# Expert layer: the 64 sample tokens' experts gathered by index and summed on VectorE, the other 512 tokens dense at 512 columns with the values summed in PSUM

## The chip, the cores and the metric

The kernel runs on one core of a Trainium2 chip. The metric is the device time of one execution in microseconds (us). The engines named below are PE (TensorE; PEld is its weight load), DVE (VectorE), ACT (ScalarE), POOL (GpSimd) and SP (SyncE, which issues the DMAs; SPq is its queue).

## The reference, cut to what matters

Two layers of a decoder trunk run for 512 prompt tokens and 64 sample tokens (576 in all), width 1024. Each layer ends in a product-key expert layer, and only that part is changed:

```python
N_KEYS, N_EXPERTS, PEER_HEADS, PEER_DK, PEER_TOPK = 128, 128 * 128, 8, 128, 16
def block(xb):
    q = (xb @ wq).reshape(blk, PEER_HEADS, 2, PEER_DK)
    s = jnp.einsum('nhpd,hpkd->nhpk', q, keys)
    s1, i1 = lax.top_k(s[:, :, 0], PEER_TOPK)
    s2, i2 = lax.top_k(s[:, :, 1], PEER_TOPK)
    cand = (s1[..., :, None] + s2[..., None, :]).reshape(blk, PEER_HEADS, PEER_TOPK * PEER_TOPK)
    cidx = (i1[..., :, None] * N_KEYS + i2[..., None, :]).reshape(blk, PEER_HEADS, PEER_TOPK * PEER_TOPK)
    sc, pos = lax.top_k(cand, PEER_TOPK)
    idx = jnp.take_along_axis(cidx, pos, axis=-1)
    g = jax.nn.softmax(sc.astype(jnp.float32), axis=-1)
    act = jax.nn.gelu(jnp.einsum('nhkd,nd->nhk', u_tab[idx], xb), approximate=False)
    return jnp.einsum('nhk,nhkd->nd', (g * act).astype(v_tab.dtype), v_tab[idx])
```

Each token picks 128 (8 heads x 16) of 16,384 experts. An expert is one row of `u_tab` and one of `v_tab`, 1024 float32 (4 KB) each.

## The kernel before

The experts are computed densely for all 576 tokens. The 16,384 experts are 128 "rows" (tiles) of 128. All large products are made of three matmuls on a high and a low float32r part (high x high, high x low, low x high). ACT casts the high part, DVE subtracts to get the low part.

**`lookup_stage`** works through 144 tiles of weights: 16 query tiles (`w_query`) and 128 tiles of `u`. A tile is loaded into one of four slots of `raw` by SP, cast to `wh` by ACT (`high`), split to `wl` by DVE (`low`), and multiplied on PE (`product`, `split_product`, L1664): 8 k-blocks x 3 parts x 2 column halves of 288 = 48 matmuls. ACT drains the result from PSUM, through Gelu into `go` for a `u` tile, and SP writes it to the DRAM tensor `activated` (`gd`). A tile's `low` is made three tiles ahead (`LEAD = 3`), and it can only be made after the tile four places earlier is used.

- The *static part* (72 tiles) has the query tiles in pairs, 2 query and 7 `u` tiles for each of 8 heads. After a query tile PE makes `scores` (L1780). DVE runs the top-16 search of a head between the `low`s, in program order: 9 `low`s for a head. At its end DVE makes the softmax weights (`found`, L2011), PE transposes indices and weights (L1819), and DVE copies them to `ix` (L2018).
- The *beats* are 72 more tiles, one with each group of 8 tokens (`GT = 8`). DVE builds one-hot rows in float16 (`one_hots`, L2033 to L2037), PE multiplies them (`sums`, L1789, 8 matmuls of 256 columns: for each token the 128x128 table of its weights, in a high and a low half), ACT copies the high halves to `wt` (L1893) and DVE adds the low halves (L2056). After four beats SP writes 2 MB of `wt` to the DRAM tensor `coefficients` (`wd`).

**`value_stage`** multiplies `activated` by `coefficients` (`weigh`), splits the result into parts, and multiplies with `v` in blocks of 8 rows: for each row 8 column groups of `v` x 3 parts x two column pieces (320 and 256) = 48 matmuls (L2145). A column group takes one and a half PSUM banks, so half the groups are worked on at a time, and after 8 rows DVE adds the sums to `h` in SBUF (`evict`, L2227). SP then writes `h` to `residual` and `y` (L2123, L2124) in two halves; the first half is written while the last half-block is computed. The stage ends when all four writes have landed, and the next layer begins.

Every stage ends in a barrier of all engines.

Of the kernel before, what the change touches and what calls it, by code (L numbers as in the profile page):

```python
# [16 lines left out]
P = 128  # L17
# [9 lines left out]
HALF = N // 2  # L27
H = 4
# [1603 lines left out]
ROWS = 8  # L1632
BLOCKS = NKEY // ROWS
STEPS = 2 * ROWS
HALVES = NKEY // 4
CH = 32
CHUNKS = N // CH
# [6 lines left out]
TILES_STATIC = 2 * PH_HEADS + U_STATIC  # L1644
TILES_ALL = 2 * PH_HEADS + NKEY
PIECES = ((0, 320), (320, 256))
# [12 lines left out]
def split_product(nc, T, out, slot, a):  # L1659

    cols = slice(a * HALF, (a + 1) * HALF)
# [5 lines left out]
    return last  # L1667


def lookup_stage(nc, T, l):  # L1670
# [4 lines left out]
    with stage(nc, "raw0", "raw1", "raw2", "raw3", "keys_in", "high", "low", "used", "drained", "scored", "kept",  # L1675
               "topped", "zeroed", "counted", "cast", "chain_v", "exp_in", "exped", "found", "turned", "tail",
               "g0", "g1", "g2", "g3", "idx_ready", "eq_ready", "rows", "summed", "halved", "evicted", "w_even", "w_odd",
               "normed", "x_high", "x_low", shared=T.bridge) as (block, s):
        raw_in = (s["raw0"], s["raw1"], s["raw2"], s["raw3"])
        g_out = (s["g0"], s["g1"], s["g2"], s["g3"])  # L1680
        w_out = (s["w_even"], s["w_odd"])

        @block.gpsimd
        def _(pool):
            nc.gpsimd.iota(T.iota[:], pattern=[[1, P]], base=0, channel_multiplier=0,
                           allow_small_or_imprecise_dtypes=True).then_inc(s["counted"], 1)

        @block.sync
        def _(sp):
# [7 lines left out]
            def load_row(r):  # L1697
                sp.dma_start(T.raw[:, b % WRING], T.d["u"][l, r]).then_inc(raw_in[b % WRING], 16)

# [3 lines left out]
            for n in range(TILES_STATIC):  # L1703
# [3 lines left out]
                if n + LEAD + WRING < TILES_STATIC:  # L1707
                    if n == 0:
                        for early in range(WRING, LEAD + WRING):
                            load_static(early)  # L1710
                    load_static(n + LEAD + WRING)
                else:
                    r = U_STATIC + n + LEAD + WRING - TILES_STATIC
                    sp.dma_start(T.raw[:, (n + LEAD) % WRING], T.d["u"][l, r]).then_inc(raw_in[(n + LEAD) % WRING], 16)
# [887 lines left out]
```

## Time and profile before

| | |
|---|---|
| time, median of 3 runs | 6484.95 us (6482.87 to 6485.23) |
| profiled execution, span of the core | 6483.6 us |
| mean granted TensorE clock | 0.974 of full speed |
| PE busy | 95% of the span |
| DVE busy | 55% |
| ACT busy | 31% |
| DMA traffic | 805.68 MB, mean 124 GB/s |

The span runs from the first to the last instruction of the profiled execution. The busy shares are averages over very different stages: the second expert layer, for example, has its dense part from 4626 to 6475 us, and within it the DVE is nearly full in some stretches and half empty in others. So the windows and the timeline of each stage say more than the page's averages.

### The profile page before, as it was taken

What the parts mean: (1) busy time and instruction counts of PE and PEld (TensorE: products, weight loads), DVE (VectorE), ACT (ScalarE), POOL (GpSimd) and SP (SyncE); (2) the same over time, 40 slices, a digit from 0 to 9 for tenths busy, and PEclk for the clock granted to TensorE, in tenths of its full rate; (3) what the DMA queues carried; (4) which work ended last, traced back from release to release, by engine and by line L of the source; (5) the groups of instructions that cost most, each with busy time, mean ns of one, the idle gap of its engine ahead of it and who ended that gap; (6) DMA issues with size and microseconds to landing.
All of it is one profiled execution on the core that took longest, in us unless ns stands there. A gap on an engine that the chain in (4) does not pass through costs nothing. (4 is left out here: it accounts for less than half of the span.)

```text
span 6483.6 us, 108190 instructions
## 1 busy us (share of the span) xinstructions
PE 6183.3 (95%) x42728; PEld 5806.5 (90%) x42728; DVE 3583.3 (55%) x6657; ACT 2014.5 (31%) x3082; POOL 0.7 (0%) x6
## 2 busy tenths in 40 slices
PE   8999988999999999999989999889999999999999
PEld 6787768989999989999967877689899999899999
DVE  3444353357788875555434443533577888755554
ACT  2223223232234442222222232232322344422222
POOL 0000000000000000000000000000000000000000
PEclk9999989999999999999999999899999999999999
DMA  3212212234446665544322122122333466655453
GB/s 105 69 51 77 70 39 78 78 121 115 117 139 176 193 196 201 181 174 171 134 98 71 50 75 71 38 79 77 124 114 116 143 179 186 207 195 182 170 175 135
DMA packets 494795, 805.68 MB, mean 124 GB/s; under 512 B 81716, under 2 KB 303156, under 8 KB 476212
## 3 DMA queue, kind: packets, MB, share of 16 engines
q1 hardware_dynamic: 494436, 800.67, 39.2%
q8 instruction: 252, 4.13, 0.3%
q14 instruction: 107, 0.88, 0.0%
HBM read 616.20 MB, written 186.72 MB: 124 GB/s over the span
## 5 line engine op out<-in xcount | busy, mean ns | idle before, releaser
L1664 PE MATMUL ps<-parts,splits 128*128 128x288 f32 x13632 | 1850.0, 296 | 0.0
L1664 PEld LDWEIGHTS ps<-parts,splits 128*128 128x128 f32 x13632 | 1812.9, 188 | 2.5
L2145 PE MATMUL ps<-parts,vh 128*128 128x320 f32 (+1 forms) x4096 | 886.4, 298 | 35.9 <-DVE splits L2216 30.7
L2145 PE MATMUL ps<-splits,vh 128*128 128x320 f32 (+1 forms) x4096 | 875.6, 295 | 0.0
L2145 PE MATMUL ps<-parts,vl 128*128 128x320 f32 (+1 forms) x4096 | 874.9, 295 | 0.0
L2221 DVE TENSOR_TENSOR vl<-third,vh 128x512 fp32r<-128x512 f32 x512 | 353.1, 690 | 671.8 <-ACT vh L2164 671.7
L2164 ACT CAST vh<-third 128x512 fp32r<-128x512 f32 x512 | 317.4, 621 | 1158.2 <-PE ps L2145 1123.6
L2145 PEld LDWEIGHTS ps<-parts,vh 128*128 128x128 f32 x4096 | 626.7, 189 | 48.9 <-issue 31.2
L2145 PEld LDWEIGHTS ps<-splits,vh 128*128 128x128 f32 x4096 | 627.9, 189 | 0.0
L2145 PEld LDWEIGHTS ps<-parts,vl 128*128 128x128 f32 x4096 | 627.6, 189 | 0.0
L163 PE MATMUL ps<-xn,wr 128*128 128x288 f32 x1952 | 495.9, 409 | 12.8 <-PEq L103 10.4
L163 PEld LDWEIGHTS ps<-xn,wr 128*128 128x128 f32 x1952 | 364.7, 191 | 125.3 <-issue 33.4
L1936 DVE TENSOR_TENSOR splits<-raw,splits 128x1024 fp32r<-128x1024 f32 x282 | 346.2, 1228 | 198.8 <-ACT splits L1843 196.8
L2056 DVE TENSOR_TENSOR wt<-wt,ps 128x1024 f32<-128x1024 f32 x144 | 335.1, 2327 | 208.7 <-ACT wt L1893 208.7
L1428 PE MATMUL ps<-parts,wmh 128*128 128x288 f32 x2048 | 413.9, 298 | 27.9 <-DVE parts L1486 27.9
L1428 PEld LDWEIGHTS ps<-parts,wmh 128*128 128x128 f32 x2048 | 330.3, 190 | 29.5 <-issue 29.5
L1893 ACT COPY wt<-ps 128x512 f32<-128x512 f32 x288 | 298.6, 1148 | 37.3 <-PE ps L1789 37.3
L1428 PE MATMUL ps<-parts,wml 128*128 128x288 f32 x1024 | 303.0, 296 | 0.0
L779 PE MATMUL ps<-xn,wr 128*128 128x288 f32 x1088 | 291.8, 415 | 11.7 <-PEq L103 9.5
L1843 ACT CAST splits<-raw 128x1024 fp32r<-128x1024 f32 x282 | 300.0, 1064 | 7.5 <-DVE second L1931 4.3
L779 PEld LDWEIGHTS ps<-xn,wr 128*128 128x128 f32 x1088 | 201.0, 194 | 66.4 <-issue 20.6
L2227 DVE SCALAR_TENSOR_TENSOR h<-ps,h 128x320 f32<-128x320 f32 (+1 forms) x384 | 184.3, 549 | 127.8 <-PE ps L2145 127.8
(378 smaller groups left out, 7682.0 us busy)
## 6 DMA issues: line engine op xcount, KB each, us to landing
raw<-in_u SPq DMA_DIRECT2D x256, 512.0 KB, 4.2
third<-in_v SPq DMA_DIRECT2D x512, 256.0 KB, 2.6
activated<-go SPq DMA_DIRECT2D x256, 288.0 KB, 4.5
coefficients<-wt SPq DMA_DIRECT2D x34, 2048.0 KB, 9.3
wr<-in_w_cm SPq DMA_DIRECT2D x104, 512.0 KB, 4.3
first<-activated SPq DMA_DIRECT2D x32, 1152.0 KB, 5.4
raw<-activated SPq DMA_DIRECT2D x32, 1152.0 KB, 5.5
wb<-coefficients SPq DMA_DIRECT2D x32, 1152.0 KB, 7.9
```

Source lines behind the costliest of these rows:

```text
L163: last = nc.tensor.matmul(bank(T, b)[:, 0:HALF], T.wr[:, slot, k, :], T.xn[:, k, a * HALF:(a + 1) * HALF], start=(k == 0), stop=(k == KD - 1))
L779: last = nc.tensor.matmul(spare(n), T.wr[:, wslot, kk, :], T.xn[:, kk, a * HALF:(a + 1) * HALF], start=(kk == 0), stop=(kk == KD - 1))
L1428: last = nc.tensor.matmul(bank(T, bank_at + a)[:, 0:HALF], wp[:, i, first + k, :], xp(k)[:, cols], start=(k == 0 and wp is T.wmh and xp is ...
L1664: last = nc.tensor.matmul(out, wp[:, slot, k, :], xp[:, k, cols], start=(k == 0 and wp is T.wh and xp is T.xh), stop=(k == KD - 1 and wp i ...
L1843: nc.scalar.copy(T.wh[:, slot], T.raw[:, slot]).then_inc(s["high"], 1)
L1893: half = nc.scalar.copy(T.wt[:, i, :, cols].rearrange("p e n -> p n e"), T.ps[:, (4 + 2 * z) * BANK:(6 + 2 * z) * BANK].rearrange("p (t z ...
L1936: nc.vector.tensor_tensor(T.wl[:, slot], T.raw[:, slot], T.wh[:, slot].bitcast(F32), ALU.subtract).then_inc(s["low"], 1)
L2056: nc.vector.tensor_tensor(rows, rows, parts[:, :, 1, :], ALU.add).then_inc(s["evicted"], 1)
L2145: last = nc.tensor.matmul(out, vp[:, x % 4, m * P:(m + 1) * P], gp[:, row, col:col + size], start=begins, stop=False, skip_group_check=True)
L2164: nc.scalar.copy(T.vh[:, x % 4], T.vr[:, x % 4]).then_inc(s["v_high"], 1)
L2221: nc.vector.tensor_tensor(T.vl[:, x % 4], T.vr[:, x % 4], T.vh[:, x % 4].bitcast(F32), ALU.subtract).then_inc(s["v_low"], 1)
L2227: add = lambda psum, dst: nc.vector.scalar_tensor_tensor(out=dst, in0=psum, scalar=1.0 / G_SCALE, in1=dst, op0=ALU.mult, op1=ALU.add)
```

## The change

The 64 sample tokens leave the dense products. The dense part keeps the 512 prompt tokens, so that a `u` tile is 24 matmuls of 512 columns in one PSUM bank (queries are still made for 576 tokens, 48 matmuls of 288), the beats are 64 instead of 72, and eight `u` tiles without a beat (`U_TAIL`) follow them. `sums` makes 16 matmuls of 128 columns: the high and the low half are added in PSUM, into one of two pairs of banks, and the DVE addition L2056 is gone. In `value_stage` a row is 24 matmuls of 512 columns, and the sums of all 128 rows stay in the eight PSUM banks until the end.

For the sample tokens POOL issues indirect DMAs: with 64 tokens x 128 experts = 8192 picks there are 64 gathers (`SLOTS`) of 128 rows of 4 KB, from `u_rows` in the lookup stage and from `v` in the value stage, into a ring of four buffers. DVE makes a dot product of each gathered `u` tile with the tokens' rows `xrow` (`dot`, one in each beat), and adds each gathered `v` tile, scaled by weight x activation, to `acc` (`blend`, one for two rows). To get `xrow`, DVE copies the tokens' columns twice (`xdup`) and PE transposes them (`turn_rows`). At the end PE adds the two halves of `acc` and transposes them (`joined`). The first row of coefficients, the first two pairs of `activated`/`coefficients` blocks, and the first `v` tiles are now prepared in the tail of the lookup stage. All four writes of `h` come after the last addition.

```diff
+            pool.wait_ge(s["indexed"], 2)
+            pool.dma_start(T.gidx[NG:P, 0:SLOTS], T.gidx[0:NG, SLOTS:2 * SLOTS]).then_inc(s["moved_i"], 16)
+            pool.dma_start(T.gw[NG:P, :], T.found[0:NG, 2, TILES - 1, SLOTS:2 * SLOTS]).then_inc(s["moved_w"], 16)
+            pool.wait_ge(s["moved_i"], 16)
+            for j in range(SLOTS):
+                if j >= GRING:
+                    pool.wait_ge(s["dotted"], j - GRING + 1)
+                gather_rows(nc, T, T.d["u_rows"], j).then_inc(u_in[j % GRING], 16)
...
+def gather_rows(nc, T, table, j):
+    return nc.gpsimd.indirect_dma_start(
+        out=T.gt[j % GRING], out_offset=None, in_=table,
+        in_offset=bass.IndirectOffsetOnAxis(ap=T.gidx[:, j:j + 1], axis=0),
+        bounds_check=DEPTH * NKEY * NKEY - 1, oob_is_err=False)
...
-                for a in range(2):
-                    last = split_product(nc, T, bank(T, 2 * par + a)[:, 0:HALF], slot, a)
-                last.then_inc(s["used"], 1)
+                split_product(nc, T, bank(T, 2 * par), slot, slice(0, ND)).then_inc(s["used"], 1)
...
-                    out = bank(T, 4 + g // 2)[:, g % 2 * 2 * P:(g % 2 + 1) * 2 * P]
-                    last = nc.tensor.matmul(out.rearrange("p (z e) -> p z e", z=2), T.oh[:, par, 0, g // 2, :, g % 2],
-                                            T.oh[:, par, 1:3, g // 2, :, g % 2], start=True, stop=True)
+                    out = tile(T.ps[:, (4 + 2 * par) * BANK:(6 + 2 * par) * BANK], g)
+                    for z in range(2):
+                        last = nc.tensor.matmul(out, T.oh[:, par, 0, g // 2, :, g % 2],
+                                                T.oh[:, par, 1 + z, g // 2, :, g % 2], start=(z == 0), stop=(z == 1))
...
+            pe.wait_ge(s["tail"], 4)
...
+            for t in range(U_TAIL):
+                product(TILES_STATIC + BEATS_ALL + t, t % 2, t % WRING)
...
-                        dve.wait_ge(s["halved"], k + 1)
-                        parts = T.ps[:, 4 * BANK:8 * BANK].rearrange("p (t z e) -> p t z e", t=GT, z=2)
-                        rows = T.wt[:, i, :, GT * b:GT * (b + 1)].rearrange("p e n -> p n e")
-                        nc.vector.tensor_tensor(rows, rows, parts[:, :, 1, :], ALU.add).then_inc(s["evicted"], 1)
+                        low(TILES_STATIC + k + LEAD, (b + LEAD) % WRING)
+                        dot(cc, i, b)
...
+            def dot(cc, i, b):
+                dve.wait_ge(u_in[b], 16 * (2 * cc) + 16 * i + 16)
+                nc.vector.scalar_tensor_tensor(
+                    out=T.gt[b], in0=T.gt[b], scalar=1.0, in1=T.xrow, op0=ALU.mult, op1=ALU.mult,
+                    accum_out=T.gact[:, bass.ds(8 * cc + BEATS * i + b, 1)]).then_inc(s["dotted"], 1)
...
+            for r in range(NKEY):
+                pe.wait_ge(s["v_low"], r + 1)
+                pe.wait_ge(s["a_low"], r + 1)
+                for m in range(KD):
+                    for vp, gp in ((T.vh, T.xh), (T.vh, T.xl), (T.vl, T.xh)):
+                        last = nc.tensor.matmul(out, vp[:, r % 4, m * P:(m + 1) * P], coef, ...)
+            pe.wait_ge(s["blended"], SLOTS)
+            pe.wait_ge(s["evicted"], 1)
...
+            def blend(p, b, first):
+                dve.wait_ge(rows_in[b], 16 * p + 16)
+                    nc.vector.scalar_tensor_tensor(out=T.acc, in0=T.gt[b], scalar=T.gact[:, bass.ds(4 * p + b, 1)],
+                                                   in1=T.acc, op0=ALU.mult, op1=ALU.add).then_inc(s["blended"], 1)
```

On PE, one beat inside the loop of the lookup stage, before (`ps` is PSUM, `parts` the tokens' high or low part, `splits` the tile's, `oh` the one-hot rows):

```order
L1664 MATMUL ps<-parts,splits 128x288 x48
L1785 REGISTER_ALU
L1789 MATMUL ps<-oh 128x256 x8
L1769 REGISTER_ALU
L1664 MATMUL ps<-parts,splits 128x288 x48
```

The same place in the changed kernel:

```order
L1667 MATMUL ps<-parts,splits 128x512 x24
L1825 REGISTER_ALU
L1830 MATMUL ps<-oh 128x128 x16
L1801 REGISTER_ALU
L1667 MATMUL ps<-parts,splits 128x512 x24
```

Half as many product matmuls, each wider; twice as many one-hot matmuls, each narrower. 

On DVE, one beat of the same loop before (`eq` and `oh` are the one-hot rows, `splits` the low part of a tile, `wt` the coefficients):

```order
L2033 TENSOR_TENSOR eq<-iota_x,ck 128x1024
L2034 TENSOR_TENSOR oh<-iota_x,ck 128x1024
L2035 REGISTER_ALU
L2036 TENSOR_TENSOR oh<-eq,ck 128x1024
L2037 TENSOR_TENSOR oh<-eq,ck 128x1024
L1935 REGISTER_ALU
L1936 TENSOR_TENSOR splits<-raw,splits 128x1024
L2056 TENSOR_TENSOR wt<-wt,ps 128x8x128
```

The same in the changed kernel (`third` holds two of the four gather buffers):

```order
L2110 TENSOR_TENSOR eq<-iota_x,ck 128x1024
L2111 TENSOR_TENSOR oh<-iota_x,ck 128x1024
L2112 REGISTER_ALU
L2113 TENSOR_TENSOR oh<-eq,ck 128x1024
L2114 TENSOR_TENSOR oh<-eq,ck 128x1024
L2005 REGISTER_ALU
L2006 TENSOR_TENSOR splits<-raw,splits 128x1024
L2118 ISA
L2118 SCALAR_TENSOR_TENSOR third,gact<-third,xrow 128x1024
```

The addition from PSUM has gone, and a dot product over a gathered tile stands in its place. On DVE between the static part and the first beat of the changed kernel:

```order
L2076 TENSOR_TENSOR t<-t,gs 128x640
L2079 TENSOR_SCALAR base<-pl 128x1
L2080 SCALAR_TENSOR_TENSOR idxf<-found 64x128
L2082 TENSOR_SCALAR gidx<-idxf,base 64x128
L2085 TENSOR_REDUCE gs<-t 128x40
L2086 RECIPROCAL gs<-gs 128x40
L2087 SCALAR_TENSOR_TENSOR found<-t,gs 128x640
L2091 COPY gw<-found 64x64
L2006 TENSOR_TENSOR splits<-raw,splits 128x1024
L2095 CAST ix<-ps 128x512 x3
L2097 TENSOR_TENSOR ix<-ps,ix 128x512
```

The four rows L2079, L2080, L2082 and L2091 are new; the rest stood there before, with 640 columns in `ix`. PE goes on with products only when L2097 is done (`tail`, 4), where before it went on after its transposes.

## Rows read from the trace of the kernel before

**Rows 1.** The page, part 1: busy time, share of the span, instructions.

```profile
PE 6183.3 (95%) x42728; PEld 5806.5 (90%) x42728; DVE 3583.3 (55%) x6657; ACT 2014.5 (31%) x3082; POOL 0.7 (0%) x6
```

**Rows 2.** Windows (head, 8 beats, values): length, busy PE, PEld, DVE, ACT, POOL; PEclk, DMA, GB/s.

```profile
4785.65:4845.13 59.48, 59.48 (x455) 59.48 (x454) 43.48 (x152) 15.47 (x21) 0.00 (x0) 1.00 0.41 115
1900.00:1958.30 58.30, 58.30 (x451) 56.78 (x450) 47.24 (x51) 28.73 (x32) 0.00 (x0) 1.00 0.63 185
2450.00:2700.00 250.00, 250.00 (x1882) 248.20 (x1880) 130.26 (x187) 71.92 (x119) 0.00 (x0) 1.00 0.51 179
```

**Rows 3.** The chain of work in order of time, around the first beat of layer 1.

```profile
5014.98 1.11 PE ps L1780 x10
...
5023.57 82.68 PE ps L1664 x624
5106.84 0.83 DVE ix L2018
5107.72 0.77 PE ps L1819 x5
5108.48 6.36 PE ps L1664 x48
5114.84 0.93 PE ps L1789 x8
```

**Rows 4.** Groups of instructions (count; busy us, mean ns of one; idle before them, releaser).

```profile
L1936 DVE TENSOR_TENSOR splits<-raw,splits 128x1024 fp32r<-128x1024 f32 x282 | 346.2, 1228 | 198.8 <-ACT splits L1843 196.8 <-DVE found L2011 0.2
L2056 DVE TENSOR_TENSOR wt<-wt,ps 128x1024 f32<-128x1024 f32 x144 | 335.1, 2327 | 208.7 <-ACT wt L1893 208.7
...
L1893 ACT COPY wt<-ps 128x512 f32<-128x512 f32 x288 | 298.6, 1148 | 37.3 <-PE ps L1789 37.3
...
L1789 PEld LDWEIGHTS ps<-oh 128*128 128x128 f16 x1152 | 100.7, 98 | 24.9
...
L2033 DVE TENSOR_TENSOR eq<-iota_x,ck 128x1024 f16<-128x1024 f16 x144 | 99.4, 690 | 1.2
...
L1780 PEld LDWEIGHTS ps<-first,second 128*128 128x128 f32 x320 | 38.8, 191 | 0.4 <-issue 0.4
```

**Rows 5.** Waits of DVE in one head's window, 4785.65 to 4845.13 (us, times, longest).

```profile
DVE splits L1936 <- ACT splits L1843: 15.6, 7, 4.3
```

**Rows 6.** Timeline of DVE at the end of the static part of layer 1.

```profile
5057.10 1.23 DVE L1936 TENSOR_TENSOR splits<-raw,splits 128x1024 fp32r<-128x1024 f32 x1 [1.53 <-ACT splits L1843]
...
5063.46 1.23 DVE L1936 TENSOR_TENSOR splits<-raw,splits 128x1024 fp32r<-128x1024 f32 x1 [2.51 <-ACT splits L1843]
...
5103.96 0.82 DVE L2011 SCALAR_TENSOR_TENSOR found<-t,gs 128x640 f32<-128x640 f32 x1
...
5106.84 2.51 DVE L2018 CAST ix<-ps 128x640 f16<-128x640 f32 x3 [0.67 <-PE ps L1819]
```

**Rows 7.** Timeline from the last beat into the value stage of layer 1.

```profile
5632.23 0.65 ACT L1887 ACTIVATE go<-ps 128x576 f32<-128x576 f32 x1 [4.33 <-PE ps L1664]
5632.90 0.33 SPq L1758 DMA_DIRECT2D activated<-go  x1
...
5639.14 1.66 ACT L2164 CAST vh<-third 128x512 fp32r<-128x512 f32 x3 [4.12 <-ACTq L2158]
```

**Rows 8.** Timeline of PE: start of layer 0's value stage, a later stall in layer 1's.

```profile
2410.85 0.82 PE L2145 MATMUL ps<-parts,vh 128*128 128x320 f32 x2 [15.34 <-DVE splits L2216]
...
5679.21 0.66 PE L2145 MATMUL ps<-parts,vh 128*128 128x320 f32 x2 [2.79 <-DVE h L2227]
```

**Rows 9.** A window of 3 us at that start, columns as in rows 2.

```profile
2411.00:2414.00 3.00, 3.00 (x13) 3.00 (x14) 2.96 (x5) 0.88 (x2) 0.00 (x0) 0.50 1.03 433
```

**Rows 10.** Timeline at the end of layer 0: PE, DVE and ACT.

```profile
3234.69 0.42 PE L2145 MATMUL ps<-parts,vl 128*128 128x320 f32 x2
...
3235.15 2.88 DVE L2227 SCALAR_TENSOR_TENSOR h<-ps,h 128x320 f32<-128x320 f32 x6 [11.29 <-PE ps L2145]
...
3249.65 1.28 ACT L266 ACT_TABLE_LOAD   x1 [26.51 <-issue]
```

More of the change, by code:

```diff
@@ L27 @@
 HALF = N // 2
+NG = NS
+ND = N - NG
 H = 4
@@ L1817, in _ @@
                     pe.wait_ge(s["tail"], 1)
-                for t in range(TILES):
-                    last = nc.tensor.transpose(tile(bank(T, 4 + 2 * (z % 2), NP_), t), T.found[:, z, t, :], T.ident)
+                for t in range(TILES - 1):
+                    last = nc.tensor.transpose(tile(bank(T, 4 + 2 * (z % 2)), t), T.found[:, z, t, :], T.ident)
                 last.then_inc(s["turned"], 1)
+            pe.wait_ge(s["tail"], 4)
             def beats(cc):
@@ L2115, in _ @@
-            with sp.Fori(1, LOOPS) as q:
-                for b in range(2):
-                    steps(2 * q + b, True, True)
-            steps(BLOCKS - 2, True, False)
-            steps(BLOCKS - 1, False, False)
+                        sp.wait_ge(s["g_tail"], 64)
+                    if not last and x in (1, 5):
+                        part = x // 4
+                        sp.wait_ge(s["a_low"], BLOCK * p + 4 * part + 4)
+                        sp.dma_start(T.gb[part], T.d["gd"][2 * p + part + 2]).then_inc(g_in[part], 16)
+                        sp.dma_start(T.wb[part], T.d["wd"][2 * p + part + 2]).then_inc(w_in[part], 16)
@@ new lines, in steps @@
+            def steps(p, first, last):
+                for x in range(BLOCK):
+                    if last and x + LEAD >= BLOCK:
+                        continue
+                    y = x + LEAD
+                    if x or not first:
+                        act.wait_ge(s["v_used"], BLOCK * p + x)
+                    if not first or y >= 4:
+                        act.wait_ge(v_in[y % 4], 32 * p + 16 * (y // 4))
+                    nc.scalar.copy(T.vh[:, y % 4], T.vr[:, y % 4]).then_inc(s["v_high"], 1)
+                    if y >= 4:
+                        act.wait_ge(s["weighed"], 2 * p + y // 4)
+                    a_high(p, y % BLOCK)
@@ new lines, in _, with steps @@
+            for x in range(1, LEAD):
+                a_low(0, x)
+            def steps(p, first, last):
+                for x in range(BLOCK):
+                    y = x + LEAD
+                    if x == 0:
+                        weigh(p, 1, None if first else 16 * p)
+                    if x == 4 and not last:
+                        weigh(p, 0, 16 * p + 16)
+                    if not last or y < BLOCK:
+                        dve.wait_ge(s["v_high"], BLOCK * p + y + 1)
+                        nc.vector.tensor_tensor(T.vl[:, y % 4], T.vr[:, y % 4], T.vh[:, y % 4].bitcast(F32),
+                                                ALU.subtract).then_inc(s["v_low"], 1)
+                        a_low(p, y)
+                    if x % 2:
+                        blend(p, x // 2, first)
```

502 lines of the change are left out of this document (239 added, 263 removed).

## The prediction

> **What bounds the kernel now.** I read the page's busy shares first: PE is busy for 95% of the span and DVE for 55% [rows 1]. A mean says little here, so I took windows of the three kinds of work that the change touches [rows 2]. In all of them PE is busy for the whole window at full clock. DVE is busy for 43.5 of 59.5 us in the search of one head, for 47.2 of 58.3 us in eight beats, and for about half of the value stage. The reader is to see that PE binds everywhere, but that DVE has only 16 us of slack in a head, and that the DMA engines are busy for 0.63 of the beats.
>
> The chain of work in order of time gives PE's prices [rows 3]: a tile of 48 matmuls of 288 columns takes 6.36 us, the 8 one-hot matmuls of a beat 0.93 us, a `scores` 1.11 us. A beat is 7.29 us.
>
> **The price of a matmul.** 6.36 us / 48 is 132.5 ns for 288 columns; at 2.4 GHz, the level of a granted clock of 1.00, the columns are 120 ns, so 12.5 ns are added. The one-hot matmuls take 116 ns for 256 columns (106.7 + 9.6). The value stage has 1882 matmuls in 250 us, 132.8 ns for 288 columns in the mean [rows 2, 3]. The addition looks constant, so I take 213.3 + 12.2 = 225.5 ns for 512 columns, and **5.41 us** for a tile of 24. If it grew with the columns (132.5 x 512/288 = 235.6 ns), the tile would be 5.65 us; that is the upper end. With nothing added it is 5.12.
>
> The Trainium skill, "TensorE: Matmul & The Clock Gate", section "Back-to-back issue gap", gives two rates for 512 columns: about 216 ns for a matmul alone, and about 131 ns for a stream of weight loads and matmuls. By the first the tile would be 5.18 us, by the second 3.14. The rows speak against the second.
>
> **The change, for one layer** (twice in the kernel):
>
> 1. *Static part.* 56 `u` tiles go from 6.36 to 5.41 us: **-53.2**. Queries and `scores` stay.
>
> 2. *Beats.* Before 72 x 7.29 = 524.9. The 16 one-hot matmuls of 128 columns are not in the trace. Lower end: 53.3 + 9.6 = 63 ns; upper end: 116 ns, if the price were that of the wider one [rows 3]. The weight load of float16 takes 98 ns where that of float32 takes 191 [rows 4], and float32 matmuls of 128 columns come every 111 ns in `scores` (10 in 1.11 us) [rows 3], so the float16 load needs some 18 ns of its own. I take 63 + 18 = 81 ns, and 1.3 us for 16, with 1.0 and 1.9 as ends. A beat is then 6.7 us; 64 of them and 8 tail tiles are 64 x 6.71 + 8 x 5.41 = 472.7: **-52.2**. For the others in a beat: DVE has 4 x 0.69 for the one-hots, 1.23 for `low`, and the dot product. That one is not in the trace; the nearest row is the 1.23 us subtraction over 1024 columns, `found` is the same kind of operation at 0.82 us for 640, which makes 1.2 to 1.3 for 1024 [rows 4, 6]. The sum is 5.3 of 6.7 us; it had been 6.3 with the 2.33 us addition. ACT has two copies of 1.15 us, a cast and a Gelu, 28.7 / 8 = 3.6 us before, and no more after [rows 2, 4]. So PE keeps the bound.
>
> 3. *Value stage.* It takes from 2410.85 to 3235.1 us before, 824.3 [rows 8, 10]. After: 128 x 5.41 = 692.5 and 1.5 for a cold start: **-130.3**. DVE has per row 1.23 (`v` low), 0.7 (coefficient low), 0.6 (a quarter of `weigh`) and half a `blend`, 0.65: 3.2 of 5.41 us. No PSUM bank is waited for until the end; the stall of 2.79 us on `h` [rows 8] is inside the 824.3.
>
> 4. *From the last beat to the value stage.* PE waits 15.34 us there, since the last coefficients go to DRAM and come back [rows 8], and then runs at a granted clock of 0.50 [rows 9]. In the changed kernel that round trip lies under the eight tail tiles (43 us), and rows 0 to 2 are ready. What is left is a Gelu of 0.65, a DMA issue of 0.33 and the barrier. Before, 6.2 us pass from the issue at 5632.90 to ACT's first work in the next stage, and two copies (2.0), an addition (2.0) and two issues (0.8) lie in them [rows 7], which leaves some 1.4 for the barrier. With 0.3 for handing over, PE waits 2.7 us. **-12.6**.
>
> 5. *Start of the lookup stage.* Eight copies of 128 columns on DVE, each about a fifth of the 0.83 us copy of 640 columns [rows 6], and eight transposes (five take 0.77 us [rows 3]): **+2.4**.
>
> 6. *The end of the search: a new stall.* DVE reaches a tile's `low` only after the tile four places earlier, so with tile 63's end (5023.57 + 5 x 6.36 = 5055.4 [rows 3]) as zero, `found` ends at 49.4 (5104.8 [rows 6]). PE reached the end of its 8 remaining tiles at 50.9, 1.5 us later, and so never waited. Now those tiles take 43.3. DVE's chain gives up little: of its wait of 2.51 us about 1, of others 0.4, so that `found` ends at 48.0 and PE stands for 4.7. Then come the transposes, a `low`, three copies and the subtraction (4.5 us), which PE now sits out (`tail`, 4); before, it lost 2.2 between its last product and the next [rows 3]. 4.7 + 4.5 - 2.2 = 7.0, and 1 for a colder clock: **+8**. Ends: 4 and 12. In the heads before, DVE's work is 59.5 - 15.6 = 43.9 us [rows 2, 5] and PE's head falls to 7 x 5.41 + 2 x 6.36 + 2 x 1.11 = 52.8, so DVE still keeps up.
>
> 7. *End of the layer.* Two of four writes of `h` (2.36 MB) are exposed before: from the end of the additions at 3238.0 to the next stage at 3249.65, 11.6 us [rows 10], some 2.4 of it fixed. Now all four are: +9.2. `joined` is 16 matmuls in float32 after the last row, each two records of 111 ns as in `scores`, 3.6 us, and one addition, against 2.9 us of additions before: +1.8. **+11**.
>
> Sum: -53.2 - 52.2 - 130.3 - 12.6 + 2.4 + 8 + 11 = -226.9 for a layer, **-454** for two. The profiled span of 6483.6 becomes 6030; the median of the runs is 1.4 us above that span, so **6031 us**.
>
> **Where the gathers hide.** In a beat a gather of 0.52 MB is added. Before, the DMA engines are busy 0.63 x 7.29 = 4.6 us in a beat. In a head 0.41 share moves 115 GB/s, so full engines would move 280 GB/s of such loads, and a gather costs 1.9 us [rows 2]: 6.4 of 6.7 us. That is nearly full, and the thinnest cover in this change. The ring of four gives each gather 27 us, so only the mean rate matters. In the value stage it is 0.51 x 6.4 + 0.9 = 4.2 of 5.41 us.
>
> **The rivals.**
>
> *The DMA engines bind the beats.* For it: 6.4 of 6.7 us, and bursts (2 MB of coefficients in pieces of 512 bytes). Against it: at another place they move 433 GB/s [rows 9]. Beats of 7.3 us, as long as before: 2 x 64 x 0.6 = +77, so 6108 us. What is late next is `dot`, then the one-hots behind it on DVE, then PE.
>
> *POOL makes the gathers too slowly.* No DMA from POOL is in the trace. Each needs 128 row addresses written while DVE is busy for 80% of the time. At 8 us a gather the lookup stage takes 2 x 64 x 1.3 = 166 more: 6197 us. This is also the case on the other side: the gain of 454 is used up when a beat is 6.7 + 454/128 = 10.2 us; at 12 us a gather the beats cost 678 and the value rows (two to a gather) 2 x 64 x 1.2 = 150 more, 6859 us. The Trainium skill, "SBUF — State Buffer", section "SBUF: two separate sides", speaks for this rival: descriptors of DMAs issued by GpSimd are written through a port that it shares with VectorE, and it is locked out while VectorE runs in a two-port mode. The float16 one-hots take 0.69 us for 1024 elements where float32 takes 1.23 [rows 4]; if that is such a mode, it is 2.8 us of each beat, and 3.9 are left. The page "DMA: Bandwidth & Descriptors", section "Anatomy of one DMA — SWDGE (gpsimd) path" of the Trainium skill would give 2.0 + 0.52/0.436 = 3.2 us for a gather, an estimate by which it stays hidden.
>
> *A stream of 512-column matmuls is far faster* (131 ns): PE would need 3.1 us a tile, and DVE would bind: about 4.9 us a tile in the search (43.9/9), 5.3 a beat and 3.2 a value row. 2 x (56 x 0.5 + 64 x 1.4 + 128 x 2.2) = 799 less, 5232 us. Against it: 288 columns already take 132.5 ns [rows 3].
>
> **How the numbers follow.** The forecast, PE bound with the prices above: 0.66. DMA-bound beats: 0.19. Slow gathers that still leave a gain: 0.11; the same past 10.2 us: 0.03. Faster matmuls: 0.01. The ends around the forecast: the one-hots at 2 x 64 x (-0.3 to +0.6) = -38 to +77; the price of 512 columns at 0.24 more or 0.29 less on 512 tiles and rows, +123 or -148; the stall of step 6 at 2 x 4 either way. Not all of them fall on one side, so I go down by 56, and up by the DMA case's 77 and some more. The range runs from 5975 to 6140 and takes in the DMA case; slow gathers and the ends together stay outside. Faster by over 0.2% (13 us, about what a measurement can tell from no change): 0.96; within it 0.01; slower 0.03.
>
> **What would show it.** The product matmuls at about 225 ns (a tile in 5.4 us); the one-hot matmuls in 1.0 to 1.9 us; a beat of 6.7 us without DVE waiting on a gather; PE idle for 4 to 5 us before the transposes and about 2 before the next product; under 3 us idle at the value stage's start; a value stage of 694 us; 20 us from the last addition to the next layer. It is wrong if `dot` waits in each beat on the gather's DMA, if POOL's issues come more than 6.7 us apart, or if the new stalls let the clock fall for long.

## The result, and the profile after

The changed kernel takes 5995.16 us (median of 4 runs, 5994.03 to 5996.48) where the kernel before takes 6484.14 (4 runs, 6482.87 to 6485.23). The ratio is 0.925, with a 95% interval of 0.9239 to 0.9261: 489 us less, where the forecast was 454 less (6031 us). The span of the profiled execution is 5994.7 us.

Page of the changed kernel, part 1, beside [rows 1]:

```profile
PE 5708.6 (95%) x31410; PEld 4859.7 (81%) x31410; DVE 3296.9 (55%) x6229; ACT 1910.5 (32%) x2798; POOL 337.5 (6%) x266
```

PE is busy for the same 95%: its work and the time shrank together. Weight loads fell from 90% to 81%. Windows of about eight beats and of the value stage of layer 1, columns as in [rows 2]:

```profile
4850.00:4901.80 51.80, 51.80 (x323) 42.72 (x322) 39.41 (x59) 28.43 (x32) 7.92 (x8) 1.00 0.91 285
5300.00:5562.00 262.00, 262.00 (x1157) 217.04 (x1156) 144.50 (x134) 75.46 (x96) 39.53 (x25) 1.00 0.66 249
```

PE is still busy for the whole of both. The DMA share of the beats rose from 0.63 to 0.91. The timeline of PE from the end of the search into the second beat, and from the last beat into the value stage, beside [rows 3, 7, 8]:

```profile
4812.51 3.13 PE L1871 MATMUL ps<-core,found 128*128 128x128 f32 x12 [3.73 <-DVEq L2090]
4817.44 7.52 PE L1667 MATMUL ps<-parts,splits 128*128 128x512 f32 x24 [1.80 <-DVE ix L2097]
4824.80 1.09 PE L1830 MATMUL ps<-oh 128*128 128x128 f16 x16
...
5230.52 1.09 PE L1830 MATMUL ps<-oh 128*128 128x128 f16 x16
5231.42 43.78 PE L1667 MATMUL ps<-parts,splits 128*128 128x512 f32 x192
5277.41 6.88 PE L2223 MATMUL ps<-parts,splits 128*128 128x512 f32 x22 [2.21 <-DVEq L2271]
```

The new stall stands in the first two rows: PE waits for `found`, and then for the last subtraction into `ix`. The last row has the stall that went: 2.21 us where 15.34 stood [rows 8]. The first tile after the stall takes 7.4 us (4817.44 to 4824.80) instead of 5.5; the windows show why, first that tile, then the beat behind it:

```profile
4817.44:4824.80 7.36, 7.36 (x24) 5.74 (x25) 7.10 (x11) 0.00 (x0) 3.27 (x3) 0.74 0.96 315
4824.80:4831.24 6.44, 6.44 (x41) 5.31 (x41) 4.83 (x7) 3.55 (x4) 0.99 (x1) 1.00 0.63 214
```

The granted clock is 0.74 in the tile behind the stall. It is a mean of two levels: the clock is at 0.50 from 4811 to 4821 us, from 2.2 us after PE's last product had ended, and then at 1.00.

```profile
4811.10:4821.20 10.10, 6.84 (x21) 5.30 (x22) 9.26 (x16) 2.90 (x4) 5.86 (x6) 0.50 0.77 232
```

So the 12 transposes also ran at the lower level: 213 ns from one start to the next, where the same transposes take 109 in r5 below. In the steady state a beat is 6.44 us (the expectations below say 6.47, an eighth of the window above, which is a little longer than eight beats). The timeline of DVE and POOL in one beat:

```profile
4851.39 0.99 POOL L1675 DMA_INDIRECT third<-in_u_rows,gidx  x1 [5.44 <-DVE third L2118]
4851.69 0.69 DVE L2110 TENSOR_TENSOR eq<-iota_x,ck 128x1024 f16<-128x1024 f16 x1 [1.09 <-PE ps L1830]
4854.69 1.23 DVE L2006 TENSOR_TENSOR splits<-raw,splits 128x1024 fp32r<-128x1024 f32 x1 [0.50 <-ACT splits L1899]
4855.83 1.22 DVE L2118 SCALAR_TENSOR_TENSOR third<-third,xrow 128x1024 f32<-128x1024 f32 x1
4857.85 0.99 POOL L1675 DMA_INDIRECT third<-in_u_rows,gidx  x1 [5.47 <-DVE third L2118]
```

POOL spends 0.99 us on a gather and then waits for 5.4 us for a free buffer; `dot` does not wait for a gather. The end of layer 0, beside [rows 10]:

```profile
2981.98 3.68 PE L2234 MATMUL ps<-core,wt 128*128 128x64 f32 x32
2985.70 0.69 DVE L2324 SCALAR_TENSOR_TENSOR h<-ps,h 128x512 f32<-128x512 f32 x1 [2.83 <-PE ps L2234]
...
3004.48 1.28 ACT L268 ACT_TABLE_LOAD   x1 [42.48 <-issue]
```

From the starts and ends of PE's matmuls, for layer 1 (layer 0 agrees within 1.5 us):

| stretch of one layer, us | before | after | change | forecast |
|---|---|---|---|---|
| first product to the last before the transposes | 477.7 | 427.5 | -50.2 | -50.8 (steps 1, 5) |
| from there to the next product | 2.0 | 8.7 | +6.7 | +7 (step 6) |
| beats and tail tiles | 524.9 | 457.8 | -67.1 | -52.2 (step 2), +1 (clock, step 6) |
| to the value stage | 15.3 | 2.2 | -13.1 | -12.6 (step 4) |
| value stage | 823.6 | 698.2 | -125.4 | -130.3 (step 3) |
| last product to the next layer (layer 0) | 14.5 | 22.3 | +7.8 | +11 (step 7) |

That makes -241 for a layer and -483 for two; nearly all of the other 6 us lie in the stages ahead of the lookup stages (about 2 us a layer) and in the first stretch of layer 0 (-51.6). No run looked into the 2 us; stages that no edit touches differ by up to 4 us between the traces below (see r7).

### The profile page after: what moved, and what is told of

Its sections match the earlier page's. It is cut to its first block and busy times, and to the rows that moved or that the text cites. A ratio compares the mean times of both kernels' runs of the same rounds, so it can differ in the third digit from the quotient of the medians.

```text
span 5994.7 us, 83802 instructions
## 1 busy us (share of the span) xinstructions
PE 5708.6 (95%) x31410; PEld 4859.7 (81%) x31410; DVE 3296.9 (55%) x6229; ACT 1910.5 (32%) x2798; POOL 337.5 (6%) x266
## 5 line engine op out<-in xcount | busy, mean ns | idle before, releaser
L1667 PE MATMUL ps<-parts,splits 128*128 128x512 f32 (+1 forms) x7488 | 1617.2, 375 | 3.6 <-DVE ix L2097 3.6
L1667 PEld LDWEIGHTS ps<-parts,splits 128*128 128x128 f32 x7488 | 1323.7, 188 | 236.3 <-issue 4.3
L2223 PE MATMUL ps<-parts,splits 128*128 128x512 f32 x6144 | 1396.5, 390 | 4.4 <-DVEq L2271 4.4
L2223 PEld LDWEIGHTS ps<-parts,splits 128*128 128x128 f32 x6144 | 1155.5, 188 | 245.4 <-DVEq L2271 5.3
L2307 DVE TENSOR_TENSOR splits<-raw,splits 128x1024 fp32r<-128x1024 f32 x250 | 306.3, 1225 | 614.8 <-ACT splits L2258 614.8
L2258 ACT CAST splits<-raw 128x1024 fp32r<-128x1024 f32 x250 | 263.3, 1053 | 961.1 <-PE ps L2223 940.2
L2006 DVE TENSOR_TENSOR splits<-raw,splits 128x1024 fp32r<-128x1024 f32 x288 | 352.9, 1225 | 230.9 <-ACT splits L1899 228.2
L1899 ACT CAST splits<-raw 128x1024 fp32r<-128x1024 f32 x288 | 305.7, 1061 | 6.9 <-DVE second L2001 4.6
L1950 ACT COPY wt<-ps 128x512 f32<-128x512 f32 x256 | 268.3, 1160 | 40.3 <-PE ps L1830 40.3
L1930 ACT ACTIVATE go<-ps 128x512 f32<-128x512 f32 x112 | 67.2, 600 | 442.2 <-PE ps L1667 442.2
L1508 DVE TENSOR_TENSOR sg<-sg,ps 128x576 f32<-128x576 f32 x48 | 36.2, 754 | 305.3 <-PE ps L1430 305.3
L1430 PEld LDWEIGHTS ps<-parts,wml 128*128 128x128 f32 x1024 | 194.5, 190 | 0.0
L1944 ACT ACTIVATE go<-ps 128x512 f32<-128x512 f32 x128 | 76.5, 598 | 346.2 <-PE ps L1667 346.2
L2110 DVE TENSOR_TENSOR eq<-iota_x,ck 128x1024 f16<-128x1024 f16 x128 | 88.6, 692 | 134.0 <-PE ps L1830 134.0
```

Source lines behind the costliest of these rows:

```text
L1430: last = nc.tensor.matmul(bank(T, bank_at + a)[:, 0:HALF], wp[:, i, first + k, :], xp(k)[:, cols], start=(k == 0 and wp is T.wmh and xp is ...
L1667: last = nc.tensor.matmul(out, wp[:, slot, k, :], xp[:, k, cols], start=(k == 0 and wp is T.wh and xp is T.xh), stop=(k == KD - 1 and wp i ...
L1899: nc.scalar.copy(T.wh[:, slot], T.raw[:, slot]).then_inc(s["high"], 1)
L1944: nc.scalar.activation(T.go[:, b], bank(T, 2 * (b % 2)), ACT.Gelu).then_inc(s["drained"], 1)
L1950: half = nc.scalar.copy(T.wt[:, i, :, cols].rearrange("p e n -> p n e"), bank(T, 4 + 2 * (b % 2) + z).rearrange("p (t e) -> p t e", t=4))
L2006: nc.vector.tensor_tensor(T.wl[:, slot], T.raw[:, slot], T.wh[:, slot].bitcast(F32), ALU.subtract).then_inc(s["low"], 1)
```

## The experiments

All are edits of the changed kernel; "the changed kernel" stands at 5995.2 us.

**r1: products of 256 columns.**

```diff
-                split_product(nc, T, bank(T, 2 * par), slot, slice(0, ND)).then_inc(s["used"], 1)
+                for a in range(2):
+                    cols = slice(a * ND // 2, (a + 1) * ND // 2)
+                    last = split_product(nc, T, bank(T, 2 * par)[:, cols], slot, cols)
+                last.then_inc(s["used"], 1)
```

> Each u product is made of 48 matmuls of 256 columns instead of 24 of 512, in the same PSUM bank; the columns, the weights and the value stage stay. Theory: a matmul costs its columns at 2.4 GHz and about 12 to 14 ns more, whatever its width. Then 128 tiles x 24 more matmuls x 2 layers = 6144 x 12.2 to 14 ns = +75 to +86 us; the stall at the end of the search gives some 5 us back, so 6065 to 6076 us, and a product tile takes 5.75 to 5.8 us against 5.45. Rival: the time goes with the columns alone, and the two 256-column halves cost nothing: 5995 us. Second rival: the gain came mainly from there being fewer matmuls, so that 256 columns cost as much above their columns as 288 did in proportion (117.8 ns each, 5.65 us a tile): +51 us, 6046 us.

Measured: 6068.03 us (6063.71 to 6071.65), +73. Two beats on PE:

```profile
5061.54 6.00 PE L1667 MATMUL ps<-parts,splits 128*128 128x256 f32 x48
5067.38 1.09 PE L1833 MATMUL ps<-oh 128*128 128x128 f16 x16
5068.28 6.00 PE L1667 MATMUL ps<-parts,splits 128*128 128x256 f32 x48
```

The beat is 6.74 us (5061.54 to 5068.28) against 6.44, with the same columns: 0.30 us for 24 more matmuls, 12.5 ns each. 2 x 128 x 0.30 = +77; the wait at the end of the search fell from 8.7 to 6.0 us, which gives 5 back: +72. So each of these float32r matmuls carries a constant of 12.5 to 13.3 ns: from start to start they take 120.0 ns at 256 columns (13.3 over the columns) and 226.7 at 512 (13.3), and the prediction had 12.5 at 288. Both rivals fall. What the constant consists of was not tried. It is not the same for every matmul: the float16 one-hot matmuls start every 57.4 ns at 128 columns, 4 ns over the columns, and every 113.6 ns at 256 (in the kernel before).

**r2: only the first four gathers of each stage.** The sample tokens' sums are left out.

```diff
-            for j in range(SLOTS):
-                if j >= GRING:
-                    pool.wait_ge(s["dotted"], j - GRING + 1)
+            for j in range(GRING):
                 gather_rows(nc, T, T.d["u_rows"], j).then_inc(u_in[j % GRING], 16)
```

> POOL issues only the first 4 of the 64 gathers in either stage; the dot products and the blends stay and work on what lies in the four buffers, so the sample tokens' sums are left out. Theory: the gathers lie wholly under PE's work, so the time stays at 5995 us within 6 us, beats stay at 6.47 us and the DMA share of a beat falls from 0.91 to about 0.7. Rival: the gathers' traffic is what lifts a 512-column matmul from the 225.5 ns forecast to 227.3 ns; then 5.41 for 5.455 us on 512 tiles and rows gives 23 us back: 5972 us. A third way: the gathers bound the beats, and without them a beat falls towards 6.2 us: 5960 us.

Measured: 5992.97 us (5992.30 to 5994.41), -2.2, less than the 3 to 4 us by which stages that no edit touches differ between traces (see r7). The beats' window:

```profile
4850.00:4901.80 51.80, 51.80 (x323) 42.70 (x322) 39.15 (x59) 28.70 (x33) 0.00 (x0) 1.00 0.70 204
```

PE does the same 323 matmuls in the same time; the value stage is 698.2 us with and without gathers. The 128 gathers of a layer cost nothing, and the 227 ns of a 512-column matmul are not their doing. A gather takes 0.21 x 6.44 = 1.4 us of the DMA share.

**r3: each gather of the lookup stage twice.**

```diff
+                if j >= 2:
+                    pool.wait_ge(more_in[j % 2], 16 * (j // 2))
+                gather_rows(nc, T, T.d["u_rows"], j, more[j % 2]).then_inc(more_in[j % 2], 16)
```

> In the lookup stage each gather is issued a second time, into two spare buffers of their own that nothing reads: 64 more gathers of 0.52 MB for a layer. Theory: the DMA engines are busy for 0.91 of a beat of 6.47 us = 5.9 us; before the change it was 0.63 x 7.29 = 4.6, so that a gather is 1.3 us, and at the price of the heads' loads 1.9. With a second gather a beat needs 7.2 to 7.8 us of the DMA engines, which then bind it: 2 x 64 x 0.7 to 1.3 = +93 to +170 us, 6088 to 6165 us. Rival: the share counts engines that have packets under way, and they could move much more (433 GB/s in another window of the kernel before, 285 here); then the beats stay at 6.47 us and the time at 5995 us. Second rival: POOL binds; its two issues are 1.0 us each of a beat, so this gives no change either unless an issue takes over 3.2 us.

Measured: 5997.51 us (5994.38 to 5998.70), no change. My theory fell. Beside the changed lines, the edit gives `gather_rows` a parameter for the spare buffer. The window:

```profile
4850.00:4901.80 51.80, 51.80 (x323) 42.72 (x322) 39.41 (x59) 28.43 (x32) 17.34 (x16) 1.00 1.03 366
```

The share went to 1.03 and the traffic from 285 to 366 GB/s, and PE and DVE waited no longer than before. A share of 0.91 does not mean that 9% are left.

**r9: the second gather, and 1 MB of writes in each beat.**

```diff
+                        for z in range(2):
+                            sp.dma_start(T.d["dump"][2 * k + z], T.xrow).then_inc(s["x_extra"], 16)
```

> The second gather of r3 stays, and in each beat SP also writes 1 MB (two times the 0.52 MB of xrow) to a DRAM tensor that nothing reads. A beat then moves 1.85 + 0.53 + 1.05 = 3.4 MB. In r3 the beats moved 366 GB/s with a DMA share of 1.03 and cost nothing, so a share near 1 is not the limit. Theory: the limit lies near the 433 GB/s that the kernel before showed in one window; 3.4 MB then take 7.9 us, and the beats get 1.4 us longer: 2 x 64 x 1.4 = +180 us, 6175 us. Rival: more is to be had (500 GB/s and over), and the beats stay at 6.47 us: 5995 to 6010 us. Second rival: reads of DRAM and writes to it hinder each other, and SP's longer queue makes the loads of u late: beats of 9 us and more, over 6300 us.

Measured: 6268.21 us (6262.44 to 6275.72), +273, half as much again as the theory's 180. A window of the beats, and what waits between 5150 and 5400 us (us, times, longest):

```profile
5150.00:5400.00 250.00, 197.61 (x1128) 160.77 (x1129) 135.52 (x204) 99.41 (x116) 74.37 (x56) 0.88 1.04 393
```

```profile
ACT go L1954 <- DMA activated<-go: 157.7, 27, 16.7
PE ps L1667 <- ACT go L1954: 56.3, 8, 9.0
```

The share is near the 1.03 of r3, but now the traffic stands at 393 GB/s without a gap. That is what this mix of transfers is held to over many beats; it is no fixed ceiling, since in r3 many slices of 1.3 us run at 394 to 427 GB/s, and 3 us ran at 433 in [rows 9]. It does not show as an even slowing: three beats of four still take 6.4 us, and the fourth 13 to 18. SP's timeline says where that time is lost:

```profile
5154.38 0.38 SPq L1764 DMA_DIRECT2D coefficients<-wt  x1
5156.54 18.13 SPq L1750 DMA_DIRECT2D raw<-in_u  x1
...
5176.52 0.33 SPq L1759 DMA_DIRECT2D activated<-go  x1
```

Behind the 2 MB write of coefficients SP stands for 18.1 us in the issue of the next load, so that the next write of `activated` is issued late, and ACT waits to reuse `go`. The same issue takes at most 2.3 us in the kernel before, 4.9 in the changed one and 7.4 in r3: there the cover became thinner without costing anything. The mean beat is 8.4 us: 2 x 64 x 2.0 = +252; the tail tiles take 51 instead of 44 us.

**r10: a slow POOL, made on purpose.**

```diff
+                for x in range(DELAY):
+                    nc.gpsimd.iota(T.idle[:], pattern=[[1, P]], base=0, channel_multiplier=0,
+                                   allow_small_or_imprecise_dtypes=True).then_inc(s["idled"], 1)
+                    pool.wait_ge(s["idled"], DELAY * j + x + 1)
```

`DELAY` is 24.

> In the lookup stage POOL runs 24 small iotas, one after the other (128x128, 0.23 us each and some 0.1 us of handing over), before it issues a gather: 7 to 9 us for a gather in place of the 1.0 us measured. This is the prediction's rival of slow gathers, made on purpose. Theory (the prediction's): with a ring of four only the mean rate matters, so the beats take on POOL's pace as soon as it is above 6.47 us, and nothing else is lost; at 8 us of pace 2 x 64 x 1.5 = +196 us, 6190 us; at 9 us +324, 6320 us. The stage's start and the value stage stay. Rival: the gather's landing (5 to 8 us) comes on top of the pace, so that a beat takes 13 us or more: over 6800 us. Second rival: the four buffers and the eight tail tiles take up the lag, and less than half of it shows.

Measured: 6354.46 us (6347.63 to 6358.03), +359. POOL in this kernel:

```profile
5199.71 1.18 POOL L1676 DMA_INDIRECT third<-in_u_rows,gidx  x1 [0.79 <-POOL idle L1710]
5200.92 7.30 POOL L1710 IOTA idle<- 128x128 f32 x24
5209.01 1.00 POOL L1676 DMA_INDIRECT second<-in_u_rows,gidx  x1 [0.79 <-POOL idle L1710]
```

POOL's pace is 9.2 us, and the mean of the beats 9.17, though single beats take 6.4 to 14.3. 2 x 64 x (9.17 - 6.44) = +349, and the tail tiles take 8 us more in a layer. The rule of the prediction holds (with a ring of four the mean rate alone counts, and it counts in full), and so does the order of its slower side: it would have come at a pace of about 10 us, ten times what a gather costs POOL.

**r4: the addition back on DVE.**

```diff
+                        dve.wait_ge(s["halved"], k + 1)
...
+                        nc.vector.tensor_tensor(rows, rows, parts[:, :, 1, :], ALU.add).then_inc(s["evicted"], 1)
```

with the 8 one-hot matmuls of 256 columns over four banks, as before the change.

> One part of the change is undone: the one-hot products are again 8 matmuls of 256 columns over four PSUM banks, ACT copies the high halves, and DVE adds the low halves; the dot product stays on DVE. Theory: DVE then has 2.41 (one-hots) + 1.14 (low) + 1.23 (dot) + 2.33 (addition) = 7.1 us for a beat and some 0.1 of handing over, while PE has 5.45 + 0.93 = 6.4; DVE binds the beats, 7.2 to 7.4 us each, 2 x 64 x 0.75 to 0.95 = +96 to +120 us: 6091 to 6115 us. Rival: the addition finds room in DVE's gaps, because the waits that stand there now go, and PE goes on binding at 6.4 us: 5986 us. Second rival: the chain addition, one-hot matmuls, ACT's copies, addition, which has only one set of banks, adds to the DVE's own work rather than lying beside it: a beat of 8 us or more, +196 us, 6190 us.

Measured: 6048.51 us (6047.61 to 6054.26), +53: the mechanism of the theory at half its size. DVE in this kernel:

```profile
4876.92 0.66 DVE L2110 TENSOR_TENSOR eq<-iota_x,ck 128x1024 f16<-128x1024 f16 x1
4877.51 0.66 DVE L2111 TENSOR_TENSOR oh<-iota_x,ck 128x1024 f16<-128x1024 f16 x1
...
4881.57 2.22 DVE L2139 TENSOR_TENSOR wt<-wt,ps 128x1024 f32<-128x1024 f32 x1
4883.72 0.66 DVE L2110 TENSOR_TENSOR eq<-iota_x,ck 128x1024 f16<-128x1024 f16 x1
```

DVE never waits, and PE waits 0.25 to 0.49 us for it in each beat: DVE binds, at 6.80 us (4876.92 to 4883.72; each fourth beat, with `pick`, 7.1). The mean of all beats is 6.84: 2 x 64 x (6.84 - 6.44) = +51. I had summed durations, but neighbouring records overlap: an operation of 2.22 us starts 2.15 before the next, one of 0.66 us 0.59. Take the pace from the starts and not from a sum of durations. Of the change itself this says that a gathered dot product on DVE had to be paid for with the addition; with both, DVE is the bound.

**r5: PE one product ahead.**

```diff
+            product(TILES_STATIC, 0, 0)
             pe.wait_ge(s["found"], 1)
...
-            pe.wait_ge(s["tail"], 4)
...
-                        product(TILES_STATIC + k, b % 2, b % WRING)
+                        product(TILES_STATIC + k + 1, (b + 1) % 2, (b + 1) % WRING)
                         sums(k, b % 2)
...
-            for t in range(U_TAIL):
+            for t in range(1, U_TAIL):
```

> PE makes the first beat's product before it waits for the end of the search, stays one product ahead in all beats, and no longer waits until the last subtraction of the indices is done. Theory: the 8.7 us between the last product of the static part and the next one lie on PE because it has nothing else to do; the product (5.45 us) covers the 3.7 us wait for the softmax weights, the next one covers the 4.4 us of copies, pick and one-hots after the transposes, and only the transposes with their waits, some 3 us, stay. 5.5 us less for a layer and 1 to 2 for the colder clock that goes too: -11 to -15 us, 5980 to 5984 us. Rival: DVE, not PE, is late there, and what PE gains it loses again at its first one-hot matmuls, since DVE's lows and one-hots come no earlier: no change, 5995 us within 3.

Measured: 5981.14 us (5977.51 to 5986.97), -14. PE at the end of the search, layer 1:

```profile
4812.23 1.03 PE L1872 MATMUL ps<-core,found 128*128 128x128 f32 x8
4813.61 0.65 PE L1872 MATMUL ps<-core,found 128*128 128x128 f32 x4 [0.35 <-DVE ix L2095]
4814.02 5.73 PE L1667 MATMUL ps<-parts,splits 128*128 128x512 f32 x24
```

The 3.73 and 1.80 us of waiting are gone, the granted clock stays at 1.00, and the tile behind them is at full speed. The lookup stages' products end 6.3 and 6.8 us earlier in the two layers, about three quarters of the 8.6 us that the stall cost. So the stall was PE's lack of work, not DVE's pace.

**r6: the first half of `h` written earlier.** The 16 matmuls of `joined` come after the third column group of the last row, and SP writes the first four rows of `h` as soon as they are complete:

```diff
+                    if ends and m == 2:
+                        join()
...
-            sp.wait_ge(s["evicted"], KD + 1)
             for g in range(2):
+                sp.wait_ge(s["evicted"], 5 + 4 * g)
```

> In the last row of the value stage the sample tokens' sums are joined (16 matmuls, 3.6 us) after the third column group instead of at the end, so that the first half of h can be written while PE makes the last four groups (2.8 us). Theory: the 14 us from the last addition to the next stage are the four writes (4.7 MB) and bound by the DMA engines; the first two start some 2.6 us earlier and the whole ends that much earlier: -4 to -6 us for two layers, 5989 to 5991 us. Rival: what ends the stage is the fixed time of the last write and not the bytes: the last two writes are issued at PE's end + 1 us either way, and nothing changes: 5995 us.

Measured: 5991.11 us (5989.97 to 5994.10), -4. That alone is no more than what untouched stages differ by (see r7); the evidence is in the stage itself: from the start of the last value stage to the end it is 714.7 us instead of 717.3, and in layer 0, from the value stage's start to the first load of the next layer, 718.1 instead of 721.0. The theory holds.

**r7: both edits.**

> Both edits of the two runs before in one kernel. Theory: they lie at different ends of the layer and add up: -15 to -21 us, 5974 to 5980 us. Rival: one of them does nothing (see there): 5980 to 5990 us.

Measured: 5972.33 us (5970.46 to 5974.06), -23, the fastest kernel here, at 0.9216 (0.9203 to 0.9228) of the kernel before. That is just below the theory's 5974 to 5980, and the two edits alone gave 18. Of the other 5 us 1.6 are the clock, which in this trace doesn't fall at the start of layer 0's value stage (693.2 us for it, where r6's trace has 694.8). The rest is not shown to be an effect: the stretch from the last product of layer 0's value stage to the first of layer 1's lookup stage, in which no edit changes more than the writes of `h`, takes 1399.1 us in the changed kernel, 1396.0 in r2 and 1403.2 in r5.

**r8: dot and blend earlier on DVE.**

```diff
-                        low(TILES_STATIC + k + LEAD, (b + LEAD) % WRING)
                         dot(cc, i, b)
+                        low(TILES_STATIC + k + LEAD, (b + LEAD) % WRING)
```

and in a value row `blend` ahead of `weigh`, `low` and coefficient part.

> On DVE the dot product goes ahead of the low part in a beat, and the blend ahead of weigh, low part and coefficient part in a value row; the work is the same. In the changed kernel POOL's issue of a gather takes 0.99 us, but 2.27 us each second time in the value stage, when the 2.28 us product of coefficients (weigh, 128x2048 float32) stands on DVE. Theory: a float32 operation on DVE with two operands in SBUF holds POOL's issue back until it ends. Now the low part (1.23 us, two float32 operands) follows dot or blend directly, so all issues in the beats get longer than 0.99 us, towards 1.3 to 1.8 us. Rival: only the long weigh does this, or only an operation that runs when the issue begins; since it never stands behind a blend any more, all issues take 0.99 us in both stages. In either case the time stays at 5995 us within 8, since the gathers have slack.

Measured: 5995.33 us (one run), no change. Groups of POOL's instructions, first of r8, then of the changed kernel (columns as in [rows 4]):

```profile
L1675 POOL DMA_INDIRECT second<-in_u_rows,gidx x64 | 78.0, 1219 | 317.0 <-DVE second L2118 305.2 <-DMA second<-in_u_rows,gidx 10.6 <-issue 1.2
L1675 POOL DMA_INDIRECT second<-in_v,gidx x64 | 66.4, 1038 | 595.2 <-DVE wt L2292 573.6 <-issue 21.6
```

```profile
L1675 POOL DMA_INDIRECT second<-in_u_rows,gidx x64 | 64.8, 1012 | 328.1 <-DVE second L2118 316.0 <-DMA second<-in_u_rows,gidx 10.9 <-issue 1.2
L1675 POOL DMA_INDIRECT second<-in_v,gidx x64 | 104.0, 1626 | 554.8 <-DVE wt L2292 533.3 <-issue 21.5
```

In the beats the issues became longer, in the value stage shorter, each where the order on DVE was changed. The last section says how.

## Why the prediction was right, point by point

*What bounds it*: right. PE is full before and after, and of the steps that rest on it the price of a matmul (columns at 2.4 GHz and a constant) is shown by r1. At 512 columns I had 225.5 ns; at full clock they take 226.7. That is most of the miss of **step 3**: 3072 matmuls at 1.2 ns more are 3.7 us a layer. The start at the lower clock, for which I had 1.5 us, costs 1.7: the granted clock is 0.50 for 3.4 us. Together the stage takes 698.2 us, 227.3 ns a matmul in the mean (the "5.455 us" of a row in the expectations), where I had 694.0. The Trainium skill, "TensorE: Matmul & The Clock Gate", section "Back-to-back issue gap", gives about 216 ns for a matmul of 512 columns alone and about 131 for a stream of loads and matmuls; the trace shows 227 in a stream.

**Step 2** is where nearly all of the 35 us come from by which the gain is larger. Its term "63 + 18 = 81 ns" for a one-hot matmul was mis-sized. A beat is 6.44 us and a tail tile 43.6 / 8 = 5.45, so 16 one-hot matmuls take 0.99 us, 62 ns each. From start to start it is 57.4 ns, below even the 63 that I had as the lower end; the rest passes at the change from one kind of matmul to the other. The weight load needs no time of its own: its record lasts 97 ns, and the matmuls start every 57. 64 x (6.71 - 6.44) = 17 us a layer. I had taken the 18 ns from the float32 matmuls of `scores`, a row of another kind.

**Step 6** was right in place and size: PE stands for 3.73 us before the transposes (forecast 4.7), the gap is 6.7 us longer (7), and the clock costs 1.9 us in the tile behind it (1). It costs over 1 us more inside the gap, since the transposes ran at the lower level; the shorter stand of PE made up for that. r5 shows that most of the stall can be avoided.

**Step 7**: +7.8 for a forecast +11. The term "9.2" was mis-sized. This is the traffic from the first write of layer 0 on, in 40 slices of 0.365 us:

```profile
GB/s 0 0 164 379 379 341 391 391 366 353 404 385 341 379 404 391 372 391 391 392 391 391 398 385 379 391 404 385 398 385 398 372 398 391 404 385 57 0 0 0
```

4.7 MB go in 12.3 us, at 385 GB/s; half as much takes 6.1, not 9.2. Of the 11.6 us of [rows 10] I had called 2.4 fixed; some 5.4 are. In the kernel before the last write lands at 3245.6, and the next layer begins 4.1 us later; in the changed kernel that part is 4.4 us.

**Step 4** came out within 0.5 us. **Steps 1 and 5** did so only in their sum, in layer 1 -50.2 us for a forecast -50.8, and that was luck. Behind the two first query tiles the static part shrank by 50.9 us, not 53.2: 56 tiles at the price of step 3's matmul, 5.44 instead of 5.41, are 1.7 us of it. The copies and transposes of step 5 cost about 0.8 us in layer 1 instead of 2.4, since only the transposes show: the time from the last product of the stage ahead to its first product did not grow (5.2 us before, 5.0 after).

*Where the gathers hide*: right that they do (r2), wrong about the margin. "6.4 of 6.7 us, nearly full" took the share of busy DMA engines for a share of what they can move. The beats moved 285 GB/s; at a mean of 366 nothing was late (r3), at 393 much was (r9), so for this mix the limit in the mean lies between. Against 393 GB/s, 2.5 MB in a beat, 1.85 were used. The DMA rival had deserved less than its 0.19. The POOL rival's price was right (r10), its condition far off: 1.0 us where it needed more than 6.4.

## What to carry to other kernels

A thin cover is judged by bytes over time against what the same mix of transfers can sustain, not by the busy share, and a short window with a higher rate (the 433 GB/s here) is no measure of that. Here the first to be late was a small write whose issue had to wait behind a large one. When an engine's work is shortened, look for the places where it used to arrive last: the wait at the end of the search had cost nothing while the products were long, costs 8.6 us a layer with the clock behind it, and most of it goes when one product is issued ahead. The float32r matmuls here cost their columns and about 13 ns each, so a full bank of 512 columns was the cheapest form tried. The 4 ns of the float16 ones say that a constant is to be read from a row of the same kind.

## What the runs showed of the hardware

POOL's issue of a gather has 128 row numbers to read from SBUF. It takes 0.99 us when DVE stands still, but 2.27 us when DVE works on `weigh`:

```profile
5865.45 2.28 DVE L2284 TENSOR_TENSOR first<-first,wb 128x2048 f32<-128x2048 f32 x1
5866.32 2.27 POOL L1675 DMA_INDIRECT third<-in_v,gidx  x1 [9.82 <-DVE wt L2292]
```

The issue ends 0.86 us after `weigh` does (5868.59 and 5867.73). In r8 it is the low part that is under way:

```profile
4854.01 1.22 DVE L2006 TENSOR_TENSOR splits<-raw,splits 128x1024 fp32r<-128x1024 f32 x1
4854.89 1.21 POOL L1675 DMA_INDIRECT third<-in_u_rows,gidx  x1 [5.23 <-DVE third L2118]
```

Again the issue ends 0.87 us after it (4856.10 and 4855.23). The kind of number does not matter: in r3 the second issue of a beat meets a float16 one-hot operation, and 114 such issues take 1.09 to 1.24 us.

```profile
4852.75 0.69 DVE L2118 TENSOR_TENSOR oh<-iota_x,ck 128x1024 f16<-128x1024 f16 x1
4853.13 1.17 POOL L1675 DMA_INDIRECT wb<-in_u_rows,gidx  x1 [0.30 <-issue]
```

But in r4, where DVE's addition under way has one operand in SBUF and the other in PSUM, 118 issues take 0.99 us:

```profile
4881.57 2.22 DVE L2139 TENSOR_TENSOR wt<-wt,ps 128x1024 f32<-128x1024 f32 x1
4882.43 0.99 POOL L1675 DMA_INDIRECT third<-in_u_rows,gidx  x1 [5.82 <-DVE third L2118]
```

So an operation of DVE with two operands in SBUF that has begun holds the issue back until it ends, and the issue ends some 0.87 us later; one that begins later does not (at 4851.69 in the changed kernel the one-hots start while an issue runs, and it takes 0.99 us). The most that such a hold cost was 1.3 us of 10.9, so it was never felt. The Trainium skill, "SBUF — State Buffer", section "SBUF: two separate sides", says that a DVE operation with two SBUF inputs, set against a GpSimd operation that reads SBUF, keeps the shared ports for its whole length, and whichever starts first has them. The traces agree where DVE starts first. Where the issue starts first they do not show it: the one-hot operation at 4851.69 lies wholly under an issue and takes its usual 0.69 us. In the prediction I had drawn on the other half of that rule, the two-port modes, and feared for the float16 one-hots; these do hold an issue back, but no more than the float32 operations with two operands in SBUF do.
